# A transformer kernel on one core: head normalisation and rotation moved beside three projections, attention queries split per unit, and one projection taken in rounded parts

## The reference, cut to what matters

```python
def queries(h):
    q = (h @ w_q).reshape(b, t, ATTN_KV_HEADS, ATTN_GROUP, HEAD_DIM).transpose(0, 2, 3, 1, 4)
    return rms_norm_2(q, q_norm)
q_l = apply_axial_rope(queries(h_lat), rope)
k_l, v_l = keys_values(h_lat)
k_l = apply_axial_rope(k_l, rope)
k_c, v_c = keys_values(h_ctx)
o_l = gqa_attend(q_l, concat(k_c, k_l), concat(v_c, v_l))   # 512 queries, 768 keys
o_c = gqa_attend(queries(h_ctx), k_c, v_c)                  # 256 queries, 256 keys
```

## Time and profile before

| what | value |
|---|---|
| median of three runs | 3610.65 us (3608.27 to 3615.75) |
| the profiled execution | 3610.93 us, its span 3609.1 us |
| TensorE busy | 3254.8 us, 90% of the span |
| VectorE busy | 1550.9 us, 43% |
| ScalarE busy | 1124.5 us, 31% |
| GpSimd busy | 535.9 us, 15% |

### The profile page before, as it was taken

How to read it: one execution, slowest core, us unless ns; L and a number is a source line. 1 busy time by engine, 2 the same in 40 slices (tenths; PEclk the granted TensorE clock), 3 DMA queues, 4 the chain that set the end, 5 groups by cost and what they waited for, 6 DMA issues and landing times. The chain is left out here.

```text
span 3609.1 us, 48582 instructions
## 1 busy us (share of the span) xinstructions
PE 3254.8 (90%) x19154; PEld 2431.0 (67%) x19154; DVE 1550.9 (43%) x2410; ACT 1124.5 (31%) x1679; POOL 535.9 (15%) x394
## 2 busy tenths in 40 slices
PE   7997957999998899988787989999998999899998
PEld 5665611576466687867566778886556888748877
DVE  5644178243224666222655332220006887723332
ACT  4213153142113333233555332220004544422321
POOL 0000022000103343250122220000004322100001
PEclk9998978999999999989798889999997999889999
DMA  3564110121230222211000011111112111112222
GB/s 132 201 250 169 59 38 0 70 95 47 94 128 24 93 94 79 89 66 65 1 1 1 24 47 70 70 47 48 50 68 75 55 69 71 51 67 93 97 84 88
DMA packets 30566, 267.90 MB, mean 74 GB/s; under 512 B 2864, under 2 KB 5296, under 8 KB 10160
## 3 DMA queue, kind: packets, MB, share of 16 engines
q1 hardware_dynamic: 30384, 265.36, 20.0%
HBM read 261.15 MB, written 4.19 MB: 74 GB/s over the span
## 5 line engine op out<-in xcount | busy, mean ns | idle before, releaser
L632 PE MATMUL banks<-normed_high,weights_high 128*128 128x512 f32 (+1 forms) x2264 | 842.0, 379 | 84.6 <-DVEq L455 47.5
L632 PE MATMUL banks<-normed_low,weights_high 128*128 128x512 f32 (+1 forms) x2264 | 831.4, 375 | 0.0
L632 PEld LDWEIGHTS banks<-normed_high,weights_high 128*128 128x128 f32 x2264 | 437.3, 193 | 192.3 <-ACT weights_high L542 41.5
L632 PE MATMUL banks<-normed_high,weights_low 128*128 128x512 f32 (+1 forms) x2264 | 544.5, 371 | 0.0
L263 DVE TENSOR_TENSOR weights_low<-ring,weights_high 128x1024 fp32r<-128x1024 f32 (+1 forms) x194 | 269.5, 1389 | 607.3 <-ACTq L555 539.2
L632 PEld LDWEIGHTS banks<-normed_low,weights_high 128*128 128x128 f32 x2264 | 438.9, 194 | 73.1 <-issue 1.2
L632 PEld LDWEIGHTS banks<-normed_high,weights_low 128*128 128x128 f32 x2264 | 405.2, 191 | 73.7
L553 ACT ACTIVATE weights_high<-ring 128x1024 fp32r<-128x1024 f32 (+1 forms) x226 | 260.9, 1154 | 618.1 <-PE banks L632 452.5
L587 POOL TENSOR_TENSOR latent_total<-latent_total,latent_square 128x512 f32<-128x512 f32 x42 | 77.1, 1836 | 1441.9 <-ACTq L530 1441.9
L632 PE MATMUL banks<-ffn_hidden,ring 128*128 128x256 f32 (+1 forms) x704 | 227.3, 486 | 1.1 <-PEq L154 1.1
L2830 PE MATMUL banks<-normed_high,hg_weights_high 128*128 128x512 f32 (+1 forms) x512 | 190.1, 371 | 15.1 <-DVEq L455 15.1
(11 more groups left out here) (539 smaller groups left out, 4787.9 us busy)
## 6 DMA issues: line engine op xcount, KB each, us to landing
ring<-in_ffn_up SPq DMA_DIRECT2D x33, 2048.0 KB, 7.5
ring<-in_ada SPq DMA_DIRECT2D x48, 1024.0 KB, 6.4
ring<-in_ffn_down SPq DMA_DIRECT2D x24, 1408.0 KB, 5.9
ring<-in_hgrn SPq DMA_DIRECT2D x16, 1536.0 KB, 6.4
ring<-in_gates SPq DMA_DIRECT2D x6, 2048.0 KB, 8.1
ring<-in_wo SPq DMA_DIRECT2D x6, 2048.0 KB, 8.0
ring<-in_w_rw SPq DMA_DIRECT2D x5, 1536.0 KB, 7.5
ring<-in_branch SPq DMA_DIRECT2D x3, 2048.0 KB, 7.8
```

The source lines that it names most:

```text
L632: mm = pe.matmul(ps[:, 0:y.shape[-1]], w, y, start=(not sweep and kk == 0 and n == 0), stop=(sweep != 0 and kk == kt - 1 and n == len(pair ...
```

## The change

It has three parts.

1. `heads_norm_rope` is gone. A class `HeadNorms` issues its operations beside the projections, through `aside`. The queries' tiles 0 to 7 come first and the two key tiles last (x = 8 and 9). During tile n of `q2`, and on into `k2`, ScalarE does the root of tile n-2 and the squares of n-1, TensorE behind the tile's own products the sums of n-1 and the swap of n-2, VectorE the norm of n-2 and the rotation of n-3. What is left goes beside `v2`, between its six parts (`by_part`): norm and rotation of the key tiles, and the splitting of the keys. The squares live in the memory of `V`, and the table of cosines is fetched in `q2`.
2. The queries are split in 96 pieces of 64 by 128, one a unit, four units ahead, in place of 16 tiles with two pieces each. Part of every turn of both loops is now `part(u + 4)`, in which VectorE waits for ScalarE's copy of the same turn.
3. In the last branch VectorE also writes the rounded and the low part of `M`, with two more operations a tile, and `w_out` takes these in place of plain float32.

```diff
+    by_part = bool(aside) and "by_part" in aside
...
-            WH = k.sb("weights_high", [P, 2, wide], stack, F32R)
-            WL = k.sb("weights_low", [P, 2, wide], stack, F32R)
+            WH = k.sb("weights_high", [P, min(2, lay.nslots * tiles), wide], stack, F32R)
+            WL = k.sb("weights_low", [P, min(2, lay.nslots * tiles), wide], stack, F32R)
...
-                        if aside and part == lay.nparts - 1:
+                        if aside and by_part:
+                            aside["tensor"](pe, part)
+                        elif aside and part == lay.nparts - 1:
                             aside["tensor"](pe, s * tiles + j)
...
+                                if name == "vector" and aside and by_part:
+                                    aside["vector"](e, part)
                                 before = e.n
                                 evac(e, at_.tile(j), part, lay.bank(at_), at_)
                                 assert e.n - before == per[j], (e.n - before, per[j])
                                 eng.sem_inc(k.emptied[name].sem, 1)
-                            if name == "vector" and aside:
+                            if name == "vector" and aside and by_part:
+                                aside["vector"](e, len(parts))
+                            if name == "vector" and aside and not by_part:
                                 aside["vector"](e, s * tiles + j)
...
-    residual_linear(k, "w_out", lambda kk: M[:, kk, :], sums=[
+    residual_linear(k, "w_out", k.H.operand(LAT), sums=[
...
+            if b == 2:
+                hi, lo = k.H.at(t, LAT)
+                e.eng.tensor_copy(hi, M[:, t, :]).then_inc(e.sem, e.tick())
+                e.eng.wait_ge(e.sem, e.now())
+                low_part(e, lo, M[:, t, :], hi)
+                e.eng.wait_ge(e.sem, e.now())
+        linear(k, f"branch{b}", [lambda kk: Y[:, kk, :]], merge, kt=MT, tiles=8, per=(1, 2, 4)[b])
...
-        linear(k, "q2", both, keep(Q), on="scalar", norms=lead)
-        linear(k, "k2", both, keep(K), tiles=2, on="scalar")
+        heads = HeadNorms(k, [(Q[:, t, :], "q_norm") for t in range(DT)] + [(K[:, t, :], "k_norm") for t in range(2)],
+                          KH, KL, V, s1)
+        linear(k, "q2", both, keep(Q), on="scalar", norms=lead, fetch=heads.fetch, aside=heads.beside(0),
+               more=dict(small_weights_loaded=16))
+        linear(k, "k2", both, keep(K), tiles=2, on="scalar", aside=heads.beside(DT))
 
         def keep_v(e, t, part, ps, at_):
             e.eng.tensor_copy(V[:, part, :], ps[:, 0:256]).then_inc(e.sem, e.tick())
             e.eng.wait_ge(e.sem, e.now())
         linear(k, "v2", [H.operand(slice(m * P, m * P + P)) for m in range(T // P)], keep_v, tiles=1,
-               weights_move=True)
-        tiles = [(K[:, t, :], "k_norm") for t in range(2)] + [(Q[:, t, :], "q_norm") for t in range(DT)]
-        heads_norm_rope(k, tiles, KH, KL)
+               weights_move=True, aside=heads.beside_values())
...
-        heads_norm_rope(k, tiles, KH, KL)
...
+QUERIES_AHEAD = 4
...
-        QS = k.sb("pa_queries", [P, 2, 2, L], s, F32R)
+        QS = k.sb("pa_queries", [P, 2 * QUERIES_AHEAD, P], s, F32R)
...
-                    if qt == 0 and p == 0:
-                        pe.wait_ge(parted.sem, parted.at(j + 1))
+                    pe.wait_ge(parted.sem, parted.at(u + 1))
...
-                def part(j):
-
-                    t, cols, keys = pairs[j]
-                    w = cols.stop - cols.start
-                    v.wait_ge(rounded.sem, rounded.at(j + 1))
-                    for p in range(2):
-                        v.tensor_tensor(QS[rows(1 - p), j % 2, p, 0:w], Q[rows(p), t, cols],
-                                        QS[rows(p), j % 2, p, 0:w].bitcast(F32), ALU.subtract).then_inc(e.sem, e.tick())
-                    v.wait_ge(e.sem, e.now())
-                    v.sem_inc(parted.sem, 1)
+                def part(u):
+                    p, x = units[u][1], u % (2 * QUERIES_AHEAD)
+                    v.wait_ge(rounded.sem, rounded.at(u + 1))
+                    v.tensor_tensor(QS[rows(1 - p), x, :], queries(u), QS[rows(p), x, :].bitcast(F32),
+                                    ALU.subtract).then_inc(parted.sem, 1)
...
-                    if u < n_units and units[u] == (first_group[groups[units[u][0]][0]], 1):
-                        j = groups[units[u][0]][0]
-                        if 1 <= j and j + 1 < n_pairs:
-                            part(j + 1)
+                    if u + QUERIES_AHEAD < n_units:
+                        part(u + QUERIES_AHEAD)
...
+                def part(u):
+                    p, x = units[u][1], u % (2 * QUERIES_AHEAD)
+                    if u >= 2 * QUERIES_AHEAD:
+                        a.wait_ge(scored.sem, scored.at(u - 2 * QUERIES_AHEAD + 1))
+                    a.activation(QS[rows(p), x, :], queries(u), ACT.Copy).then_inc(rounded.sem, 1)
...
+class HeadNorms:
+    def __init__(self, k, tiles, KH, KL, V, stack):
...
+        self.SQ = V[:].rearrange("p m n -> p (m n)").rearrange("p (b n) -> p b n", b=2)
+        self.RT, self.ROPE = k.sb("head_turned", [P, L], stack)[:], k.sb("head_cos_sin", [P, 2, L], stack)[:]
...
+    def sums(self, pe, x):
+        pe.wait_ge(self.squared.sem, self.squared.at(x + 1))
+        if x:
+            pe.wait_ge(self.logged.sem, self.logged.at(x))
+        for c in range(2):
+            mm = pe.matmul(self.k.PS[4 + c][:, 0:T // 2], self.k.const("pair"), self.SQ[:, x % 2, c * T // 2:(c + 1) * T // 2])
+        mm.then_inc(self.summed.sem, 1)
...
+    def beside(self, first):
+        def by_scalar(e, n):
+            if n == 0:
+                e.eng.preload_act_table_set("natural_log_exp_and_others")
+            if n + first >= 2:
+                self.root(e, n + first - 2)
+            if n + first >= 1:
+                self.square(e, n + first - 1)
+        def by_tensor(pe, n):
+            if n + first >= 1:
+                self.sums(pe, n + first - 1)
+            if n + first >= 2:
+                self.swap(pe, n + first - 2)
+        def by_vector(e, n):
+            if n + first >= 2:
+                self.norm(e, n + first - 2)
+            if n + first >= 3:
+                self.rope(e, n + first - 3)
+        return dict(scalar=by_scalar, tensor=by_tensor, vector=by_vector)
+    def beside_values(self):
+        def by_scalar(e, n):
+            e.eng.preload_act_table_set("natural_log_exp_and_others")
+            self.root(e, DT)
+            self.square(e, DT + 1)
+            self.root(e, DT + 1)
+            for m in range(2):
+                self.keys_high(e, m)
+        def by_tensor(pe, part):
+            if part == 0:
+                self.sums(pe, DT + 1)
+            if part in (1, 2):
+                self.swap(pe, DT + part - 1)
+        def by_vector(e, part):
+            if part == 0:
+                self.norm(e, DT)
+                self.rope(e, DT - 1)
+            if part == 2:
+                self.norm(e, DT + 1)
+            if part in (3, 4):
+                self.rope(e, DT + part - 3)
+            if part >= 5:
+                self.keys_low(e, part - 5)
+        return dict(scalar=by_scalar, tensor=by_tensor, vector=by_vector, by_part=True)
```

More of the change, by code:

```diff
@@ L2361, in of, with queries @@
             return g, p, j, qt, t, cols, keys
+        def queries(u):
+            g, p, j, qt, t, cols, keys = of(u)
+            return Q[rows(p), t, cols.start + qt * P:cols.start + qt * P + P]
         def split_at(keys):
@@ L2468, in low @@
                                     ALU.subtract).then_inc(low_taken.sem, 1)
-                part(0)
-                part(1)
+                for u in range(QUERIES_AHEAD):
+                    part(u)
                 maximum(0)
```

184 lines of the change are left out of this document (65 added, 119 removed).

## The result

The changed kernel takes 3628.95 us, the median of 6 runs (3625.38 to 3631.90), against 3611.87 for the kernel before on the same chip, also of 6: 17.1 us slower. One of those six took 4577.98 us and is left out of the ratio, 1.005 [1.0038, 1.0063]; the median of the other five is 3610.65, which makes the loss 18.3. The forecast was 3619.5 in a range of 3606 to 3641, with 0.62 on slower, so the loss is about twice the 9 us that were forecast.

What follows compares the result with a forecast made beforehand. TensorE, busy 90% of the span, was taken as the bound, with attention a chain of hand-overs. Terms -5.6 - 25.4 - 2.1 + 33.4 + 4.4 + 4.0 = +8.7 us gave 3619.5 us, range 3606 to 3641.

Steps and rivals of the forecast that it cites:

- likeliest case: Whole kernel: ScalarE and VectorE alternate in attention and outweigh the gains elsewhere, 3611 to 3629 us, chance 0.58.
- w_out, to q2's first matmul: w_out stage: three rounded products save 11.2 us, less what comes back, -5.6 us (-9 to -5).
- head work, q2's first matmul to attention's first copy: q2, k2 and v2: +18.2 us of TensorE head work, -43.6 us before attention begins, sum -25.4 (-29 to -20).
- latent units, with the clock's 4: Attention's 64 latent units: +33.4 us from engines going in turns, +4 for a lowered TensorE clock.
- context units: Attention's context units: a cycle of 2.12 us makes 67.1 us against 62.7, +4.4 (+1 to +8).
- Its three terms: w_out costs coming back: stage start 1.8 us, last tile's merge 1.3, low clock after the pause 2.5.
- the walk: v2 followed step by step from ScalarE's weights: attention begins at 34.0 us instead of 77.6, TensorE waiting 0.6, then until 15.6.
- the cycle: Latent units: ScalarE and VectorE wait for each other's current turn, 3.41 us a unit (3.3 to 3.5) against 2.92.
- The clock that falls in the lockstep: Rival, latent units: TensorE at half rate for half the units adds 20 us instead of 4, 3636 us; chance 0.15.
- No lockstep: Rival, attention: copies ready when VectorE asks, latent units at 2.57 us each, 162 in all, about 3556 us; chance 0.12.
- Cancelling: Rival, whole kernel: gains in the stages and losses in attention cancel, about 3609 to 3613 us; chance 0.12.
- Stalls of q2: Rival, v2 or q2: ScalarE's root late in each tile, 1 us each, 3628 us; chance 0.03.

Runs made afterwards that it cites:

- VectorE one behind: Changed kernel, but VectorE subtracts in each turn the query piece that ScalarE copied a turn earlier: 3568.54 us, 0.987 of the kernel before.
- outputs a turn later: VectorE one behind, plus VectorE's low part of each output one turn after ScalarE's high part: 3537.14 us, 0.9795 of the kernel before.
- piece ahead of the inverse: VectorE one behind, plus its small subtraction issued ahead of the reciprocal that releases GpSimd: 3556.64 us.
- fastest kernel: Outputs a turn later, plus v2's key-tile work on VectorE one part earlier and the piece ahead of the inverse: 3522.65 us, 0.9751 of the kernel before.
- part 3 alone: Kernel before with only the changed attention (queries split in pieces), head stage and w_out as they were: 3656.56 us, 1.0125 of the kernel before.

## Why the prediction was right, and where its terms were off

The sign and the mechanism were right: the gains outside attention are eaten by a lockstep of ScalarE and VectorE in it. The size was not: the loss is about twice the forecast's, because a small difference of large terms was to be told. The median lies 9.5 us above the forecast, in the range and at the edge of the likeliest case's own 3611 to 3629. Term by term, measured in the trace:

| term | forecast | measured |
|---|---|---|
| w_out, to q2's first matmul | -5.6 | -5.8 |
| head work, q2's first matmul to attention's first copy | -25.4 | -25.7 |
| first copy to first exponential | -2.1 | -2.2 |
| latent units, with the clock's 4 | +37.4 | +38.8 |
| context units | +4.4 | +9.3 |
| last exponential to wo2's table load | 0 | +1.8 |
| sum at wo2's start | +8.7 | +16.2 |

The later stages are 1.7 us shorter in the profiled execution, which leaves +14.5 of span. The medians are 17.1 apart. What lengthened the end of attention by 1.8, which the forecast put at nothing, no run takes apart.

*Part 1.* Its three terms came out as said. TensorE's idle time at the start is 5.01 against 2.04, 3.0 more, and it holds two of them, the last merge and the start of the stage. VectorE's last step of the merge and ScalarE's table load, before:

```profile
904.71 0.69 DVE L869 TENSOR_TENSOR merged<-merged,gated 128x512 f32<-128x512 f32 x1
905.79 1.28 ACT L653 ACT_TABLE_LOAD   x1 [30.11 <-PEq L154]
```

and after:

```profile
905.83 0.69 DVE L263 TENSOR_TENSOR normed_low<-merged,normed_high 128x512 fp32r<-128x512 f32 x1
906.92 1.28 ACT L656 ACT_TABLE_LOAD   x1 [31.29 <-PEq L154]
```

The merge, with its copy (0.43) and subtraction (0.69), ends 1.12 us later and the stage begins as much later, 1.2 counted from the branch's last matmul, where 1.3 was said. From the table load the first matmul is 908.89 - 906.92 = 1.97 us away, where it was 0.19: 1.8, as said. The products took 8.8 less, where 11.2 less 2.5 for the clock was said. That is right by two errors: the low clock at the start cost 1.4 (the first product takes 7.01 us, the others 5.60), and the other 1.1 is that a product takes 5.60 here and not the 5.47 of k2.

*Part 2.* v2 takes 34.39 us in the profiled execution where the walk gave 34.0 (the walk has full clock; at the low one in tile 9's sums, which most kernels here show, it takes 35.9), q2 and k2 17.5 more where 18.2 was said. The two waits of TensorE in v2 that the walk gave, 0.6 and 1.3 us, are in the trace: 0.65 in front of tile 9's sums, in the row at 1690.34 above, and 1.17 in front of its swap:

```profile
1699.66 1.12 PE L2619 MATMUL banks<-gq_keys,constants 128*128 128x512 f32 x2 [1.17 <-DVEq L2613]
```

Of the table load the rows above show 1.28 us and the next operation 0.01 behind its end. The drain of 1.38 us that the Trainium skill, "ScalarE: Activation LUTs", section "What ACT_TABLE_LOAD costs", adds to a switch of sets doesn't show here either, where the set in use is loaded again. The page gives the drain for a switch to a different set, so the forecast's "By the page v2 would be 1.4 longer" went beyond it.

*Part 3, the cycle.* Forecast 3.41 us, measured 3.50 and 3.43 in alternation, a mean of 3.46. By its steps in the rows above, and in brackets in the turn behind it: exponential to copy 1827.98 - 1826.20 = 1.78 and (1.60), where 1.65 was said; copy and hand-over 0.34 (0.33), said 0.38; subtraction to maximum 0.21 (0.31), said 0.20; maximum's start to exponential 1.17 (1.18), said 1.18. The two kinds of turn differ in that the copy of the transposed block waits 0.17 us behind the exponential's sum in the one, and the subtraction and the maximum do not overlap in the other. The 61 intervals are 3.7 us above the 207.4 of the sum, which had also rounded 3.41 to 3.4. The seven outputs came 1.1 us over the cycle each and not 0.85, 1.7 us more. Together that is 5.4 above the 33.4. The 4.0 set aside for the clock cost nothing: the clock did fall in single turns, but the turn at 0.55 in the rows above kept to 3.50. So the 38.8 lies near the forecast's 37.4 by two errors.

*Part 3, the context units.* This is the term that was sized worst, by 4.9 us. The formula took the pace of the short unit from the start. The first six intervals behind the last latent exponential are 2.89, 2.55, 2.47, 2.22, 2.15 and 3.25, 15.5 us where six cycles of 2.12 make 12.7: the first three turns still hold latent units' transposed blocks, and the sixth a latent output. The cycle itself is 2.15 and 2.22, in the mean 0.05 more than said, 1.3 us in all; the last two intervals took 0.6 more and the outputs 0.2 more than said. The forecast counts 31 intervals where there are 32, in both its terms, which cancels but for 0.1. It gave this stage no clock term, rightly: the granted clock is 0.65 here and was 0.68 before, and the cycle is the same at either of its two levels, 1.2 and 2.4 GHz. Two intervals of the changed kernel:

```profile
1979.09:1981.24 2.15, 1.09 (x6) 0.90 (x8) 1.12 (x7) 1.04 (x5) 0.48 (x1) 0.50 0.00 0
1983.46:1985.61 2.15, 1.09 (x12) 0.89 (x12) 1.12 (x7) 1.04 (x5) 0.48 (x1) 0.97 0.00 0
```

At the low clock part of TensorE's matmuls fall into the next turn, which has it busy for 2.13 of its 2.22 us, and it still keeps up.

*The rivals.* The clock that falls in the lockstep is refuted for the latent units by its mean, 0.93 against 0.91, and by the constant cycle. No lockstep is refuted by the 93 waits. Its price was right for the latent units alone: with the lockstep and the outputs' wait gone they take 159.8 us, where 162 was said. The kernel is at 3537 and not at 3556 mainly because of the context units, on which the rival had nothing and which take 49.9 in place of 64.8. A small misreading stands in the 2.57: of the seven splittings six are 5.7 us apart and the last, of a context tile, 4.8, which makes the other turns 2.59. Cancelling: the measured gains and losses don't. Stalls of q2: none, its stage is 0.7 us shorter than said.

*The expectation of VectorE one behind* was the worst number of the study, 155 for 178.6 us of latent units. I had found the same-turn wait of the pieces and priced an output as work alone, although the forecast itself had them "on the cycle, ScalarE's copy and then VectorE's subtraction". The outputs a turn later gave 18.8 of the 23.6 us back, and the piece ahead of the inverse 4.5 more.

## What to carry to other kernels

When two engines hand work to each other in a loop, ask of each pair of instructions which turn the producer issues it in, not how many units ahead the data are: a lead of four or eight units is worth nothing if both sides handle the unit in the same turn, and a shift of one side by one turn, with the same instructions, gave 60 us of 3629 (each beside its own runs of before: 65). When such a wait is found, look for every other pair of the same form in the loop, here the outputs, whose shift gave some 30 us more (3568.54 to 3537.14, each beside its own runs of before: 27). And a piece of work that is too coarse (six splittings of 5.7 us each and one of 4.8) may be cheaper than its fine version (a wait in every turn), until the turns are shifted.

## What the runs showed of the hardware

*VectorE's small subtraction is held up by GpSimd.* With VectorE one unit behind, the same instruction takes 0.284 to 0.786 us. GpSimd, scaling the probabilities in the kernel with VectorE one behind, and then VectorE:

```profile
1785.86 0.91 POOL L2508 TENSOR_SCALAR pa_probs<-pa_probs,pa_inverse 128x768 f32<-128x768 f32 x1 [2.20 <-DVE pa_inverse L2466]
1789.59 0.91 POOL L2508 TENSOR_SCALAR pa_probs<-pa_probs,pa_inverse 128x768 f32<-128x768 f32 x1 [2.83 <-DVE pa_inverse L2466]
```

```profile
1788.04 0.29 DVE L2452 TENSOR_TENSOR pa_queries<-gq_queries,pa_queries 64x128 fp32r<-64x128 f32 x1
...
1789.85 0.78 DVE L2452 TENSOR_TENSOR pa_queries<-gq_queries,pa_queries 64x128 fp32r<-64x128 f32 x1
1790.66 0.96 DVE L2459 TENSOR_REDUCE pa_max<-banks 128x1 f32<-128x768 f32 x1
```

At 1788.04 GpSimd is idle, and the subtraction takes 0.29. At 1789.85 GpSimd has been at work since 1789.59 and ends at 1790.50; the subtraction ends at 1790.63. So it ends 0.13 us behind GpSimd's operation, and the maximum behind it is late by half a microsecond. It is no single case: 47 of the 96 subtractions take over 0.30 us in this trace, and each of them starts during an operation of GpSimd and ends 0.13 to 0.14 us behind it. With the subtraction ahead of the reciprocal that releases GpSimd, all 96 take 0.284 to 0.290, and latent and context units are 4.5 and 2.3 us shorter. The Trainium skill, "SBUF — State Buffer", section "SBUF: two separate sides", states this: VectorE and GpSimd share a port pair as an exclusive lock for a whole instruction, and a VectorE operation with two SBUF inputs falls under it against a GpSimd operation that reads SBUF. The subtraction is such an operation, and the trace agrees.

*One piece of work fell on either level of the clock.* Tile 9's sums in v2, behind 0.65 us of waiting and eight matmuls at full rate, ran at 0.50 in eight of nine profiled executions and at 1.00 in the changed kernel's own, 1.4 us apart. A forecast of a stretch with such short waits is no finer than that, and one profiled execution may not be the usual one.

*The granted clock changed with the order of work, and in the lockstep it cost next to nothing.* TensorE is busy for 48.5 of 64.8 us at a granted 0.68 in the kernel before, for 47.1 of 74.1 at 0.65 in the changed one, and with the outputs a turn later for 32.7 of 49.8 at 1.00; with VectorE one behind alone the clock is 0.80, in the fastest kernel 0.96. At a low clock the same matmuls are busy for longer, so these shares are not the same amount of work. In the lockstep the low clock is nearly free, as the two intervals of 2.15 us show; in the kernel with part 3 alone two latent turns took 3.8 us, one at 0.65 and one behind a turn at 0.50. What it costs where the engines no longer wait for each other no run here isolates.
